# The residual's gate moved from the combine stage to the experts' eviction, and eight PSUM banks in place of four for the next stage's projections

## The reference, cut to what matters

```python
def first_block(...):
    ...
    sh1, sc1, gt1, sh2, sc2, gt2 = jnp.split(mod[:, None, :], N_MOD, axis=-1)
    ...
    x = x + gt1 * mix
    h2 = rms_norm(x, g_norm2[l]) * (1.0 + sc2) + sh2
    x = x + gt2 * hier_moe(h2, ...)      # top 2 of 32 experts for each token
    return rms_norm(x, g_final)

def hier_moe(...):
    ...                                   # each row's two experts and weights w0, w1
    return (jax.nn.silu(xblk @ w_gate[e]) * (xblk @ w_up[e])) @ w_down[e]   # a row of an expert
    out = jnp.zeros(...).at[buf_tok].add(yb * buf_w[:, None])               # w0 * y0 + w1 * y1

def second_block(x, ...):
    h = jnp.concatenate([meta, x], axis=1)          # 16 meta tokens, then 512
    hn = _rmsnorm(h, norm_mix_pre[l])
    proj = hn_p @ w_in[l]                           # sb_q, sb_k, sb_v, ...
    sb = _stick_breaking(...)
    ...
```

## Time and profile before

| | us |
|---|---|
| median of 3 runs | 1932.29 |
| lowest and highest of them | 1927.04, 1932.38 |
| the profiled execution | 1924.79 |
| its span in the profile | 1923.0 |
| PE busy | 1759.9 (92%) |
| PE weight loads busy | 1353.9 (70%) |
| DVE busy | 803.9 (42%) |
| ACT busy | 590.3 (31%) |
| mean granted TensorE clock | 0.971 of full speed |

### The profile page before, as it was taken

How to read it: one execution, slowest core, us unless ns; L and a number is a source line. 1 busy time by engine, 2 the same in 40 slices (tenths; PEclk the granted TensorE clock), 3 DMA queues, 4 the chain that set the end, 5 groups by cost and what they waited for, 6 DMA issues and landing times. The chain is left out here.

```text
span 1923.0 us, 27361 instructions
## 1 busy us (share of the span) xinstructions
PE 1759.9 (92%) x11698; PEld 1353.9 (70%) x11698; DVE 803.9 (42%) x1351; ACT 590.3 (31%) x988; POOL 61.5 (3%) x86
## 2 busy tenths in 40 slices
PE   6999989999989988738999899989999989999997
PEld 3883445666655655427765699889998889999886
DVE  3865566111110110144357467343236545444333
ACT  4323422100000000045557533443323333232222
POOL 1001000000000000020000000000000000000000
PEclk9999989999999999978899899899999999999999
DMA  9856525899999999951110111122233032322321
GB/s 371 273 170 192 228 102 197 336 427 425 427 428 427 426 427 427 416 191 41 38 45 23 45 45 35 54 67 88 88 97 123 1 99 89 109 89 88 110 88 44
DMA packets 111217, 355.38 MB, mean 185 GB/s; under 512 B 8663, under 2 KB 71405, under 8 KB 97399
## 3 DMA queue, kind: packets, MB, share of 16 engines
q1 hardware_dynamic: 106342, 343.89, 46.8%
q0 software_dynamic: 4224, 9.33, 1.4%
q10 hardware_dynamic: 530, 0.40, 0.1%
HBM read 330.21 MB, written 23.33 MB: 184 GB/s over the span
## 5 line engine op out<-in xcount | busy, mean ns | idle before, releaser
L1663 PE MATMUL psum<-parts_memory 128*128 128x256 f32 (+3 forms) x1136 | 346.8, 305 | 10.6 <-PEq L1882 3.3
L1665 PE MATMUL psum<-parts_memory 128*128 128x256 f32 (+3 forms) x1136 | 342.8, 302 | 0.0
L1664 PE MATMUL psum<-parts_memory 128*128 128x256 f32 (+3 forms) x1136 | 342.7, 302 | 0.0
L1562 DVE TENSOR_TENSOR parts_memory<-fixed,parts_memory 128x1024 fp32r<-128x1024 f32 x139 | 166.9, 1222 | 212.1 <-ACT parts_memory L1554 212.1
L1663 PEld LDWEIGHTS psum<-parts_memory 128*128 128x128 f32 x1136 | 218.0, 192 | 20.5 <-DVE parts_memory L1562 4.6
L1664 PEld LDWEIGHTS psum<-parts_memory 128*128 128x128 f32 x1136 | 217.9, 192 | 7.0
L1665 PEld LDWEIGHTS psum<-parts_memory 128*128 128x128 f32 x1136 | 217.5, 191 | 6.8
L1663 PE MATMUL psum<-mix_parts,parts_memory 128*128 128x256 f32 (+2 forms) x664 | 206.4, 311 | 4.7 <-PEq L2613 4.0
L1664 PE MATMUL psum<-mix_parts,parts_memory 128*128 128x256 f32 (+2 forms) x664 | 207.1, 312 | 0.0
L1665 PE MATMUL psum<-mix_parts,parts_memory 128*128 128x256 f32 (+2 forms) x664 | 206.4, 311 | 0.0
L1554 ACT ACTIVATE parts_memory<-fixed 128x1024 fp32r<-128x1024 f32 x139 | 143.2, 1055 | 120.7 <-PE psum L1665 109.6
(11 more groups left out here) (414 smaller groups left out, 2387.3 us busy)
## 6 DMA issues: line engine op xcount, KB each, us to landing
fixed<-in_w_exp_gate_dram SPq DMA_DIRECT2D x19, 2048.0 KB, 29.8
fixed<-in_w_exp_up_dram SPq DMA_DIRECT2D x19, 2048.0 KB, 31.1
fixed<-in_w_exp_down_dram SPq DMA_DIRECT2D x19, 2048.0 KB, 31.4
fixed<-in_w_in_dram SPq DMA_DIRECT2D x36, 1024.0 KB, 5.4
attention_memory<-in_w_exp_up_dram SPq DMA_DIRECT2D x14, 2048.0 KB, 31.1
attention_memory<-in_w_exp_down_dram SPq DMA_DIRECT2D x14, 2048.0 KB, 31.4
attention_memory<-in_w_exp_gate_dram SPq DMA_DIRECT2D x14, 2048.0 KB, 29.8
fixed<-in_w_mod_dram SPq DMA_DIRECT2D x8, 2048.0 KB, 9.0
```

Of the source, the lines that this page charges most:

```text
L1562: dve.tensor_tensor(out, raw, high.bitcast(F32), ALU.subtract).then_inc(self.low_ok, 1)
L1663: pe.matmul(out, x(0), w(0), start=start, stop=False)
L1664: pe.matmul(out, x(0), w(1), start=False, stop=False)
L1665: return pe.matmul(out, x(1), w(0), start=False, stop=stop)
```

## The change

There are three edits, in four places. The gate is copied in another layout, half its columns on each half of the partitions, and `take_y` multiplies by it while it moves rows out of PSUM. In the combine stage `weigh` and the gate's multiplication go; `mix` becomes two operations, each of which adds one weighted row to the residual, and waits for the gathers itself. In the next stage the projections of `outputs` go over eight banks in the order 4, 5, 6, 7, 0, 1, 2, 3, and wait for `taken` only from n = 8 on; the row projections behind them keep four banks (`row_bank`).

```diff
-        step(dve.tensor_copy(g["gt2"], modacc[:, 5120:6144]))
+        for h in range(2):
+            rows = slice(BR * h, BR * h + BR)
+            step(dve.tensor_copy(g["gt2"][rows, 0:512], modacc[rows, 5120 + 512 * h:5632 + 512 * h]))
...
-                dve.tensor_copy(yb[j], psum[:, BY, :]).then_inc(y_sb, 1)
+                dve.tensor_tensor(yb[j], psum[:, BY, :], g["gt2"][:, 0:512], ALU.mult).then_inc(y_sb, 1)
...
         def mix(t):
-            y0, y1 = y[:, 2 * t, :], y[:, 2 * t + 1, :]
-            dve.wait_ge(weighted, t + 1)
-            step(dve.scalar_tensor_tensor(out=y0, in0=y1, scalar=weight[:, 2 * t + 1:2 * t + 2], in1=y0,
-                                          op0=ALU.mult, op1=ALU.add))
-            step(dve.tensor_tensor(y0, y0, gt2, ALU.mult))
-            dve.tensor_tensor(res[:, t, :], res[:, t, :], y0, ALU.add).then_inc(mixed, 1)
+            first, second = (dict(out=res[:, t, :], in0=y[:, i, :], scalar=weight[:, i:i + 1], in1=res[:, t, :],
+                                  op0=ALU.mult, op1=ALU.add) for i in (2 * t, 2 * t + 1))
+            dve.wait_ge(y_in[t], 32)
+            step(dve.scalar_tensor_tensor(**first))
+            dve.scalar_tensor_tensor(**second).then_inc(mixed, 1)
...
-        def weigh(t):
-            act.wait_ge(y_in[t], 32)
-            y0 = y[:, 2 * t, :]
-            act.activation(y0, y0, ACT.Copy, scale=weight[:, 2 * t:2 * t + 1]).then_inc(weighted, 1)
...
-    BANKS = [4, 5, 6, 7]
+    BANKS = [4, 5, 6, 7, 0, 1, 2, 3]
+    row_bank = lambda n: 4 + n % 4
...
-                pe.wait_ge(taken, n - 3)
+                if n >= 8:
+                    pe.wait_ge(taken, n - 7)
                 lo, width = columns_of(first, i)
-                turned(pe, psum[:, BANKS[n % 4], 0:width], w, x, lo, width).then_inc(ready, 1)
+                turned(pe, psum[:, BANKS[n % 8], 0:width], w, x, lo, width).then_inc(ready, 1)
```

More of the change, by code:

```diff
@@ L1687, in combine @@
     parts, hnP = g["parts"], g["hnP"]
-    gt2 = g["gt2"]
     y = g["ring"].rearrange("p s n -> p (s n)")[:, RAW_SLOTS * RAW:RAW_SLOTS * RAW + 8 * D].rearrange("p (i n) -> p i n", i=2 * TT)
@@ L1694, in combine @@
     y_in, loads = [dma_sem(f"rows_gathered{t}") for t in range(TT)], dma_sem("final_gain_loaded")
-    weighted, mixed, dstep = sem("rows_weighted"), sem("rows_mixed"), sem("combine_dve_step")
+    mixed, dstep = sem("rows_mixed"), sem("combine_dve_step")
     eps_col = small[:, 56:57]
@@ L1809, in finish_act @@
         take(0)
-        weigh(0)
         for t in range(TT + 2):
-            if t + 1 < TT:
-                weigh(t + 1)
             if t < TT:
@@ L1921, in project_rows @@
                     for k in range(4):
-                        last = three(pe, psum[:, BANKS[n % 4], 0:256], lambda part: hnP[:, part, 4 * j + k, cols],
+                        last = three(pe, psum[:, row_bank(n), 0:256], lambda part: hnP[:, part, 4 * j + k, cols],
                                      lambda part: w(part)[:, k, :], j + k == 0, j == 1 and k == 3)
@@ L2018, in take_projection @@
                 act.wait_ge(ready, n + 1)
-                bank = psum[:, BANKS[n % 4], :]
+                bank = psum[:, BANKS[n % 8], :]
                 lo, width = columns_of(first, half)
@@ L2041, in take_rows @@
                 rows = P if t < TT else META
-                act.activation(v[0:rows, t, c * 256:(c + 1) * 256], psum[0:rows, BANKS[n % 4], 0:256], ACT.Copy).then_inc(taken, 1)
+                act.activation(v[0:rows, t, c * 256:(c + 1) * 256], psum[0:rows, row_bank(n), 0:256], ACT.Copy).then_inc(taken, 1)
             for n in range(len(outputs)):
```

## The result

| | before | after |
|---|---|---|
| median | 1931.78 (4 runs, 1927.04 to 1932.38) | 1919.70 (4 runs, 1917.96 to 1920.92) |
| profiled execution | 1924.79, span 1923.0 | 1917.96, span 1916.2 |
| granted clock, mean | 0.971 | 0.973 |

The ratio is 0.9942, 95% interval 0.9924 to 0.9960. The median lies inside the stated range and 5.3 us under the 1925.0 that was forecast. The two profiled spans differ by 6.8 us, the medians by 12.1. So a comparison of two traces does not explain the whole difference, and neither does the sum of 5.9.

What follows compares the result with a forecast made beforehand. DMA was taken to bound the experts' stage, VectorE the combine stage, TensorE what follows. Terms 0 + 0 - 4.8 - 1.1 give -5.9 us; with most of the median's excess over its runs removed, 1925.0 us, range 1918 to 1931.5.

Steps and rivals of the forecast that it cites:

- the sum of 5.9: Whole kernel: gate copy 0, eviction 0, combine-stage mixes 4.8 and projection banks 1.1 us, together 5.9 us less.
- Parts 1 and 2: Routing stage's gate copy, 0.2 us more but covered by VectorE's idle time; experts' eviction multiplies for free: 0 us each.
- Part 3: Combine stage: two operations per mix instead of three, and an earlier start, bring the barrier 4.8 us earlier (bounds 3.6 to 6.0).
- Part 4: Barrier after the combine stage: n = 4 no longer waits for ScalarE, 1.1 us saved (bounds 0 to 1.8).
- rival A: First projections: TensorE's clock rises later after the shorter combine, costing up to 12.0 us, time 1938.4; chance 0.08.
- B (given back later): After the barrier: a later step with its own time absorbs the 5.9 us, leaving 1930.6 to 1932.3; chance 0.12.
- C (no gain from the banks): At the barrier something else holds TensorE's start, so only the mixes gain: 4.8 us, 1927.5; chance 0.08.
- D (more than the sum): Gathers come earlier, or the clock falls less often later: 8 to 10 us gained, 1922 to 1924; chance 0.10.

Runs made afterwards that it cites:

- banks only: The kernel before with only the change to eight PSUM banks, old gate and mixes kept; ratio 0.9971, mean -5.0 ± 0.9 us against before.
- mixes only: The changed kernel with the old four banks, so only the gate's move and two-operation mixes; ratio 0.9968, mean -7.0 ± 1.2 us against before.
- after again: The changed kernel, nothing altered, timed once more beside the kernel before on another chip; ratio 0.9961, mean -7.6 ± 1.2 us against before.
- before again: The kernel before, nothing altered, timed under a label of its own; ratio 0.9992, mean -1.4 ± 1.2 us against before.

## Why the prediction was right, and where it was off

**Parts 1 and 2, the gate.** The eviction takes 692 ns with the factor, 692 without. The copies take 0.87 us instead of 0.69, 0.18 more where 0.2 was taken, ahead of VectorE's idle time. Right.

**Part 3, the mixes.** Mix to mix is 848.01 - 844.76 = 3.25 us with the wait, and mix(1) follows the landing. B is 36.0 to 37.1 us in the nine traces with the new mixes in this order, 36.4 in the mean, and 41.2, 41.4 and 41.1 in three with the old ones, 41.2: 4.8 us, as in the sum. From the landing to the first projection it is 868.55 - 844.76 = 23.8 us, where 24.2 was forecast. The wait before mix(1) was 0.58 us instead of 1.15, since this execution's gathers for tile 1 came 3.25 us behind those of tile 0, and not 3.67. In the eight traces with the new mixes and no unused matmuls the wait was 0.6 to 1.6 us. Right in place and size. What the sum had no term for is C, where 1.0 of B's gain went back in this pair of traces: 0.7 with fifteen low matmuls instead of eight, and 0.3 at the barrier. The 0.7 has the mechanism of rival A, at a small part of its price of 12 us. That the earlier stage causes it is not shown, since before's own combine stage had 5, 8 and 20 low matmuls in three traces. The rise of the clock moved by 3 us against the first projection in these three, more than the "some tenths" of a microsecond that the prediction allowed. Over all traces B and C together fell by 4.1 us, from 56.0 in both traces of before to 52.0 in the mean of eight; against banks only's 57.1 it is 5.1.

**Part 4, the banks.** D is 37.5 us in both traces of before, 36.2 and 36.3 with the banks: 1.2 to 1.3, where the sum had 1.1. TensorE's own distance at the barrier went from 2.92 us to 1.97 and 2.00 instead of the 1.8 forecast, and ScalarE's wait for n = 9 is gone. The term was sized from the one trace in which the clock had stayed up behind the barrier. In three of five traces with the wait it fell, and D was 39.0 and 40.1 with the one-taking wait. So a part of the sum is missing, of up to 2.6 us in an execution.

**The sum.** -5.9 was forecast and 6.8 is the difference of the two traces, of which only B, C and D, -5.3, are the change's. The difference of the means over all executions is 8.1 ± 0.8. The 12.1 between the medians of the result is far outside of this: that set's four executions of before have a mean of 1930.75, 1.8 above the 1929.0 of all 83, and the four of the changed kernel lie 1.3 below their mean of ten. With four executions each, the difference of the means there is 11.2 ± 1.4. So part of the 5.3 us by which the forecast was beaten is the luck of these eight executions, which the prediction had named as a possibility and left in its range.

**What stays open.** 8.1 less 5.9 is 2.2 ± 0.8. The clock's falls behind the barrier could be it. But the run that takes away the idle time and keeps the wait gained nothing in its mean over the run with the bare wait, and the banks alone measured 5.0 where their own stretch shows 1.2. The parts do not add up in the means either: 7.0 and 5.0 alone, 8.1 together.

The record has one more number for each execution, its mean granted clock. A straight line of time against clock, with one slope for the 181 executions of the four sets and a level of its own for each kernel and each set, has 1.3 us for each 0.001 and brings the scatter down from 2.8 to 1.2 us. At equal clock the difference to before is 3.2 ± 0.5 us for mixes only, 2.0 ± 0.5 for banks only, 5.5 ± 0.6 for after again, 5.2 ± 0.6 without the gate, and none for before again (+0.5 ± 0.5). Now the parts add up, 3.2 and 2.0 to the 5.5 of both, and the traces' 5.3 fits. So what the raw means have above the sum came with a higher mean clock: banks only ran at 0.9712 on average and before beside it at 0.9688. The line takes away more than luck, though. A combine stage that is 5 us shorter has 5 us less at half clock, which lifts the mean clock by 0.0013 and would be 1.7 us of the line, without a matmul running faster; and a fall of the clock that the change avoids is a gain of the change. So what the change is worth lies, as far as this shows, between 5.5 and 8.1 us. Since the clock is on record only as one number for each span, except for one trace of each kernel, I can't say in which stretch the other executions differ, nor whether the banks keep the clock up there.

**The rivals.** B (given back later) is out: the stretch E is the same within what two traces of before differ by, and the means show the gain. The expectation of mixes only says that the bank edit's 1.2 us were given back before 946 us. TensorE's same 52 matmuls behind D show what that was, first in before, then in before once more, then after:

```profile
932.58:946.08 13.50, 11.80 (x52) 7.64 (x53) 6.85 (x20) 8.08 (x6) 0.00 (x0) 0.62 0.13 38
933.00:948.05 15.05, 13.34 (x52) 9.11 (x53) 8.01 (x22) 8.08 (x6) 0.00 (x0) 0.55 0.12 33
924.23:938.75 14.52, 12.80 (x52) 8.58 (x53) 7.46 (x22) 8.08 (x6) 0.00 (x0) 0.57 0.13 35
```

They took 13.50 us at a mean clock of 0.62 in the first, and 15.05 at 0.55 in the second, which has no bank edit. So the first trace of before was lucky there, and no gain of the edit was given back. C (no gain from the banks) is out by D in the traces, and by 2.0 ± 0.5 at equal clock. D (more than the sum) is what happened in the raw means, and not by earlier gathers; that the clock falls less often is one of its two conditions, and is shown in place in the traces with the wait, but not sized.

## What to carry to other kernels

When one engine's row of operations fills a stage, count its operations per tile: three to two was worth 1.2 us a tile here, and the first tile's saving went into a wait for the transfer behind it. Here a wait at a barrier, with TensorE's matmuls 3.2 us apart, cost its length of 1.3 us and in both traces another 1.5 to 2.6 us by the clock behind it; so size such a term from more than one trace. Where means differ by less than a kernel's own scatter (3 us here), read the change from stretches between two fixed instructions, and the luck from the stretches that it doesn't touch; and set the times against the mean clock of each execution before a surplus is put down to the change.

## What the runs showed of the hardware that I had not expected

Equal code gives spans that differ by 12.6 us (1921.6 to 1934.2 us in 94 executions of before), and within a kernel the time goes down by 0.9 to 1.7 us for each 0.001 of the granted clock's mean. TensorE's clock did not always fall after the same idle time: after 2.94 us in the routing stage it was 1.00 over the next 16 us in one trace, 0.89 in another. How many matmuls of the first projection ran at the low level differed from 5 to 20 in three traces with one and the same combine stage. And matmuls that compute nothing of use shortened the combine stage by 1.8 us.
